# State-space stage: input projections of x, B and C as seven half-size products from the third group on

## The reference, cut to what matters

```python
zxbcdt = x @ w_in                      # x: 256 x 1024; w_in: 1024 x 6176
z = zxbcdt[..., :2048]
xbc = zxbcdt[..., 2048:2048 + 4096]    # x: 2048 columns, B: 1024, C: 1024
dt_raw = zxbcdt[..., 6144:]
xbc = silu(causal_depthwise_conv(xbc, conv_w, conv_b))   # 4 taps along the tokens
xs, bm, cm = xbc[..., :2048], xbc[..., 2048:3072], xbc[..., 3072:]
...
y = ssd_chunked(xh, dt, a, bm, cm) + d_skip * xh         # per group: 4 heads of 64, state 128, 2 chunks of 128
yg = y * silu(z); yg = yg * rsqrt(mean(yg ** 2, per group) + eps)
out = yg @ w_out
```

## Time and profile before

| | before |
|---|---|
| median of 3 runs | 1808.0 us |
| span of the profiled execution | 1806.1 us |
| TensorE busy | 1786.0 us, 99% |
| VectorE busy | 721.9 us, 40% |
| ScalarE busy | 448.2 us, 25% |
| GpSimd busy | 70.9 us, 4% |
| HBM read | 524.91 MB, 291 GB/s over the span |

### The profile page before, as it was taken

How to read it: one execution, slowest core, us unless ns; L and a number is a source line. 1 busy time by engine, 2 the same in 40 slices (tenths; PEclk the granted TensorE clock), 3 DMA queues, 4 the chain that set the end, 5 groups by cost and what they waited for, 6 DMA issues and landing times.

```text
span 1806.1 us, 21261 instructions
## 1 busy us (share of the span) xinstructions
PE 1786.0 (99%) x8612; PEld 984.0 (54%) x8647; DVE 721.9 (40%) x1667; ACT 448.2 (25%) x958; POOL 70.9 (4%) x66
## 2 busy tenths in 40 slices
PE   9999999999999999999999999999999999999999
PEld 8888754443443333455444344343366767568874
DVE  3566754212221213035421221221345566234675
ACT  2332312111111100133210111110134534217780
POOL 0000000000000000000000000000011110001110
PEclk9999999999999999999999999999999999999999
DMA  9723569999999999708899999999942332041520
GB/s 389 305 83 139 193 254 410 420 427 428 426 428 429 427 427 425 309 1 349 357 425 428 428 427 427 428 427 427 425 162 94 140 123 110 7 181 47 236 91 23
DMA packets 41828, 527.41 MB, mean 292 GB/s; under 512 B 4800, under 2 KB 5472, under 8 KB 8576
## 3 DMA queue, kind: packets, MB, share of 16 engines
q1 hardware_dynamic: 39200, 516.70, 68.7%
q10 hardware_dynamic: 2528, 9.31, 1.3%
HBM read 524.91 MB, written 1.08 MB: 291 GB/s over the span
## 4 chain that ended last, share of the span: by engine, by line
PE 88%; DMA 9%; DVE 2%; SPq 1%; ACT 0%; issue 0%; POOL 0%; DVEq 0%; ACTq 0%
PE ps L212 32%; PE ps L876 20%; PE ps L911 10%; DMA ring<-in_wu 6%; PE ps L810 4%; PE ps L928 3%; PE ps L715 2%; DMA ring<-in_w_lat 2%; PE ps L1702 2%; PE ps L1670 2%; PE ps L1234 1%; PE ps L679 1%; PE ps L1717 1%; PE ps L883 1%; PE ps L1446 1%; PE ps L1459 1%
## 5 line engine op out<-in xcount | busy, mean ns | idle before, releaser
L876 PE MATMUL ps<-ring,work 128*64 128x512 f32 x1856 | 409.1, 593 | 6.0 <-DMA ring<-in_wu 5.7
L212 PE MATMUL ps<-xl,ring 128*128 128x256 f32 (+3 forms) x1344 | 291.5, 375 | 0.4 <-DMA ring<-in_w_x 0.4
L876 PEld LDWEIGHTS ps<-ring,work 128*64 128x64 f32 x1856 | 131.6, 137 | 270.7 <-issue 251.2
L212 PEld LDWEIGHTS ps<-xl,ring 128*128 128x128 f32 x1344 | 243.7, 190 | 39.5 <-issue 2.5
L911 PE MATMUL ps<-ring,work 128*64 128x512 f32 x816 | 181.5, 594 | 0.1
L212 PE MATMUL ps<-ring,xl 128*128 128x256 f32 (+1 forms) x576 | 176.0, 463 | 0.2 <-ACT xl L1787 0.2
L2647 DVE TENSOR_TENSOR work<-work,ps 128x512 f32<-128x512 f32 x32 | 22.0, 688 | 361.4 <-PE ps L876 341.7
L212 PEld LDWEIGHTS ps<-ring,xl 128*128 128x128 f32 x576 | 108.3, 190 | 59.3 <-issue 49.9
L911 PEld LDWEIGHTS ps<-ring,work 128*64 128x64 f32 x816 | 56.2, 137 | 100.3 <-issue 98.7
L3178 POOL TENSOR_TENSOR small<-small,halves 128x1 f32<-128x1 f32 (+4 forms) x42 | 45.7, 1087 | 1545.7 <-DVE small L2449 936.6
L2608 DVE SCALAR_TENSOR_TENSOR work<-ps,small,big 128x512 f32<-128x512 f32 x60 | 45.0, 750 | 135.8 <-ACT big L1918 135.8
(11 more groups left out here) (476 smaller groups left out, 1958.9 us busy)
## 6 DMA issues: line engine op xcount, KB each, us to landing
ring<-in_wg SPq DMA_DIRECT2D x62, 2048.0 KB, 20.6
ring<-in_wu SPq DMA_DIRECT2D x52, 2048.0 KB, 21.7
ring<-in_wd SPq DMA_DIRECT2D x48, 2048.0 KB, 22.0
xl<-in_wd SPq DMA_DIRECT2D x10, 2048.0 KB, 23.5
xl<-in_wu SPq DMA_DIRECT2D x9, 2048.0 KB, 19.1
ring<-in_w_odd SPq DMA_DIRECT2D x8, 2048.0 KB, 7.4
ring<-in_w_xz SPq DMA_DIRECT2D x7, 2048.0 KB, 22.9
ring<-in_w_qkv SPq DMA_DIRECT2D x6, 2048.0 KB, 34.3
```

The lines of the kernel that those rows point to most:

```text
L212: i = e.matmul(bout, lhs(k), rhs(k), start=start and k == ks[0], stop=stop and k == ks[-1])
L876: last = e.matmul(b[64 * j:64 * j + 64, :], x[:, 4 * a + k, 64 * j:64 * j + 64], w[k // 2][:, 2 * (k % 2) + j, :], start=a + k == 0, stop= ...
```

## The change

The two blocks of a half, the two halves of the 256 tokens and the two halves of the 1024 features form a 2 x 2 by 2 x 2 product of matrices. From the third group on (`FAST = 2`) it is made of seven half-size products in place of eight (Winograd's form), each of 4 matmuls with 128 moving columns in place of 256: 28 matmuls of half the width per half, where there were 16.

- **GpSimd** makes the four sums of x once (`pool_x_sums`), and for each half four sums of weights of 512 elements a row, two groups ahead (`pool_sums`), one of them in place in the ring. They stand in its queue ahead of the power that y's norm needs.
- **TensorE** makes three products into ps5 (`part_mm`), then four into ps2 or ps3 (`mm_conv`). The first three of a half wait for `first_sums` of the half before, since they share ps5.
- **VectorE** adds the products up: copy and sum out of ps5, then three sums with the other bank, into `raw` in SBUF, and convolves from `raw` back into the products' bank. In the groups 1 to 6 the convolution of half 0 stands behind the decay products now, and in the groups 0 to 6 the second block of half 1 behind the gate.
- **ScalarE** takes the SiLU from the banks, one half at a time, for the groups from the third on.
- **The ring** gives one slot ("half") to the sums, from the start until `mm_conv(7, 1)`. "sum" is given out later, and the output weights are loaded in another order. What the loads near the seam of mixer and experts wait for:

| chunk, in SyncE's order before | waited for | waits for now |
|---|---|---|
| wo(0,0) | z of group 3 | the same |
| wo(1,1) | z of 4 | half 1 of 5 (third now) |
| wo(0,1) | half 1 of 5 | z of 4 (second now) |
| wo(1,0) | z of 5 | z of 6 |
| mg(0,0) | z of 6 | half 1 of 7 |
| mu(0,0), mu(0,1) | half 1 of 7, z of 7 | the same |
| md(0,0) | p5 | c21 |
| mg(1,0) | c21 | p7 |
| mg(1,1) | p3 | p3, behind mg(1,0) |
| mu(1,0), 1536 KB of it | z of 7 | the same, behind the others |
| mu(1,1) | p7 | p5, behind the others |
| md(1,0), then the first half of mg(0,1) | p4, p4 | the same |

From md(1,1) on the first layer's loads wait for the same steps of the experts as before.

```diff
+FAST = 2
...
+            if g == 1:
+                ring.add(("half",), 0, mm_conv(7, 1))
+                ring.order.remove(ring.chunks["half",][0])
+        WO = [(0, 0, "c21"), (0, 1, "p7"), (1, 1, "p3"), (1, 0, "p4")]
         for hf, n, last in WO:
+            if (hf, n) == (1, 0):
+                ring.add(("sum",), 0, out_mm("p5"))
             ring.add(("wo", hf, n), 1, out_mm(last))
+        ring.order.insert(1, ring.chunks["half",][0])
...
+        halfv = ring.view("half")
+        wsums = [area(halfv, 1536 * i, (3, 4, 128)) for i in range(2)]
+        xsums = [area(xl, 2048, (4, 128)), area(xl, 2560, (4, 128)), area(halfv, 3072, (4, 128)), area(halfv, 3584, (4, 128))]
+        raw = area(big, 3584, (4, 128))
+        def wq(g, half, j, h_):
+            v = kview(8, 512)(ring.view("BC", g // 2) if half else ring.view("w", g))
+            c = 256 * j + 128 * (g % 2) if half else 256 + 128 * j
+            return v[:, 4 * h_:4 * h_ + 4, c:c + 128]
+        def xq(h_, c):
+            return xS[:, 4 * h_:4 * h_ + 4, 128 * c:128 * c + 128]
...
+            if half < 2 and g >= FAST:
+                tensor_seven(e, g, half, j)
+            elif half < 2:
...
+        def tensor_seven(e, g, half, j):
+            x, y = ps[5], ps[2 + half]
+            s1, s2, s4 = (wsums[half][:, i] for i in range(3))
+            t1, t2, t3, t4 = xsums
+            def product(b, at, w, x_):
+                for k in range(4):
+                    last = e.matmul(b[:, 128 * at:128 * at + 128], w[:, k, :], x_[:, k, :], start=k == 0, stop=k == 3)
+                return last
+            if j == 0:
+                e.wait_ge(*(ring("BC", g // 2) if half else ring("w", g)))
+                if half:
+                    e.wait_ge(*first_sums(g, 0))
+                else:
+                    e.wait_ge(*(first_sums(g - 1, 1) if g > FAST else dec_d(0, 1)))
+                product(x, 0, wq(g, half, 0, 0), xq(0, 0))
+                product(x, 1, wq(g, half, 0, 1), xq(1, 0))
+                e.wait_ge(*sums_in(g, half))
+                product(x, 2, s2, t2).then_inc(*part_mm.up(g, half))
+            else:
+                e.wait_ge(*(cs_in(g - 1) if g > FAST else conv(g - 1, half)))
+                product(y, 1, s1, t1)
+                product(y, 2, wq(g, half, 1, 0), t3)
+                product(y, 0, wq(g, half, 1, 1), t4)
+                product(y, 3, s4, xq(1, 1)).then_inc(*mm_conv.up(g, half))
...
-            e.wait_ge(*conv(g, 1))
-            if g > 1:
-                e.wait_ge(*mm_off(g - 2))
-            e.activation(cs[:, g % 2], cv, ACT.Silu).then_inc(*cs_in.up(g))
+            if g < FAST:
+                e.wait_ge(*conv(g, 1))
+                e.activation(cs[:, g % 2], cv, ACT.Silu).then_inc(*cs_in.up(g))
+                return
+            e.wait_ge(*mm_off(g - 2))
+            for half in range(2):
+                e.wait_ge(*conv(g, half))
+                i = e.activation(cs[:, g % 2, 2 * half:2 * half + 2].rearrange("p a n -> p (a n)"), ps[2 + half][:, :], ACT.Silu)
+                i.then_inc(*(cs_in.up(g) if half else as_.up()))
...
-        def vector_conv(e, g, half):
-
+        def vector_conv(e, g, half, blocks=(0, 1)):
+            if g >= FAST and 0 in blocks:
+                x = ps[5][:, :].rearrange("p (a n) -> p a n", a=4)
+                y = ps[2 + half][:, :].rearrange("p (a n) -> p a n", a=4)
+                e.wait_ge(*part_mm(g, half))
+                e.tensor_copy(raw[:, 1], x[:, 0]).then_inc(*vs.up())
+                e.wait_ge(*vs())
+                e.tensor_tensor(raw[:, 0:4:2], bc(raw[:, 1], 1, 2), x[:, 1:3], ALU.add).then_inc(*first_sums.up(g, half))
+                e.wait_ge(*first_sums(g, half))
+                e.wait_ge(*mm_conv(g, half))
+                e.tensor_tensor(raw[:, 1:4:2], bc(raw[:, 2], 1, 2), y[:, 1:3], ALU.add).then_inc(*vs.up())
+                e.wait_ge(*vs())
+                e.tensor_tensor(raw[:, 1], raw[:, 1], y[:, 3], ALU.add).then_inc(*vs.up())
+                e.tensor_tensor(raw[:, 2:4], bc(raw[:, 3], 1, 2), y[:, 0:2], ALU.add).then_inc(*vs.up())
+                e.wait_ge(*vs())
             e.wait_ge(*mm_conv(g, half))
             if g:
                 e.wait_ge(*cs_in(g - 1))
-            for j in range(2):
+            for j in blocks:
                 blk = 2 * g + j if half == 0 else 16 + 8 * j + g
-                b = ps[2 + half][:, j * 256:(j + 1) * 256]
-                o = cv[:, 2 * half + j, :]
+                b, o = ps[2 + half][:, j * 256:(j + 1) * 256], cv[:, 2 * half + j, :]
+                if g >= FAST:
+                    b, o = raw[:, 2 * j:2 * j + 2].rearrange("p a n -> p (a n)"), b
...
-                if g < 7:
-                    vector_conv(e, g + 1, 0)
                 if g == 0:
+                    vector_conv(e, 1, 0)
                     for t in range(2):
                         e.wait_ge(*mm_seg(t))
                         e.tensor_tensor(dec[:, t], ps[4 + t][:, :].rearrange("p (h l) -> p h l", h=4),
...
                     e.wait_ge(*dec_e(g, t))
                     e.tensor_tensor(dec[:, t], dec[:, t], bc(ps[1][:, 128 + 128 * t:256 + 128 * t], 1, 4),
                                     ALU.mult).then_inc(*(vs.up() if t == 0 else dec_in.up(g)))
+                if 0 < g < 7:
+                    vector_conv(e, g + 1, 0)
                 if g < 7:
-                    vector_conv(e, g + 1, 1)
+                    vector_conv(e, g + 1, 1, (0,))
                 else:
                     vector_mix(e)
                 e.wait_ge(*mm_y(g))
...
                 e.wait_ge(*vs())
                 e.wait_ge(*zs_in(g))
                 e.tensor_tensor(yv, yv, zs[:, i], ALU.mult).then_inc(*gated.up(g))
+                if g < 7:
+                    vector_conv(e, g + 1, 1, (1,))
...
+        def pool_x_sums(e):
+            t1, t2, t3, t4 = xsums
+            e.wait_ge(x_in[0], 16)
+            e.wait_ge(x_in[1], 16)
+            e.wait_ge(*mm_conv(0, 1))
+            e.tensor_tensor(t1, xq(0, 1), xq(0, 0), ALU.subtract).then_inc(*gs.up())
+            e.wait_ge(*gs())
+            e.tensor_tensor(t2, xq(1, 1), t1, ALU.subtract).then_inc(*gs.up())
+            e.tensor_tensor(t3, xq(1, 1), xq(0, 1), ALU.subtract).then_inc(*gs.up())
+            e.wait_ge(*gs())
+            e.tensor_tensor(t4, xq(1, 0), t2, ALU.subtract).then_inc(*sums_in.up("x"))
+        def pool_sums(e, g, half):
+            s1, s2, s4 = (wsums[half][:, i] for i in range(3))
+            e.wait_ge(*(ring("BC", g // 2) if half else ring("w", g)))
+            e.wait_ge(*mm_conv(g - 1, half))
+            e.tensor_tensor(s1, wq(g, half, 1, 0), wq(g, half, 1, 1), ALU.add).then_inc(*gs.up())
+            e.wait_ge(*gs())
+            e.tensor_tensor(s2, s1, wq(g, half, 0, 0), ALU.subtract).then_inc(*gs.up())
+            e.tensor_tensor(wq(g, half, 1, 0), wq(g, half, 0, 0), wq(g, half, 1, 0), ALU.subtract).then_inc(*gs.up())
+            e.wait_ge(*gs())
+            e.tensor_tensor(s4, wq(g, half, 0, 1), s2, ALU.subtract).then_inc(*sums_in.up(g, half))
         def gpsimd(e):
+            pool_x_sums(e)
             for g in range(8):
+                if g + 2 < 8:
+                    for half in range(2):
+                        pool_sums(e, g + 2, half)
```

More of the change, by code:

```diff
@@ L279, in build @@
         qkT_in = Sig(sem("qkT_in"), qkT_mm.keys)
-        sc_mm, sc_max, sc_exp = sig("sc_mm", H8, range(2)), sig("sc_max", H8), sig("sc_exp", H8, range(2))
+        part_mm = sig("part_mm", range(FAST, 8), range(2))
+        first_sums = sig("first_sums", range(FAST, 8), range(2))
+        sc_mm, sc_max, sc_exp = then(part_mm, H8, range(2)), then(first_sums, H8), sig("sc_exp", H8, range(2))
         p_in, pT_mm, pT_in, av_mm, av_in = (sig(n, H8) for n in ("p_in", "pT_mm", "pT_in", "av_mm", "av_in"))
-        sl_var, sl_rs, sl_in = (sig(n, range(2), range(2)) for n in ("sl_var", "sl_rs", "sl_in"))
+        sums_in = Sig(sem("sums_in"), [("x",)] + each(range(FAST, 8), range(2)))
+        sl_rs = then(sums_in, range(2), range(2))
+        sl_var, sl_in = (sig(n, range(2), range(2)) for n in ("sl_var", "sl_in"))
         oT_mm, oT_in = sig("oT_mm", range(2), range(2)), sig("oT_in", range(2), range(2))
```

3 lines of the change are left out of this document (removed).

## The result

| | before | after |
|---|---|---|
| median | 1807.6 us | 1820.7 us (1819.6 to 1821.2) |
| span of the profiled execution | 1806.1 us | 1819.1 us |
| VectorE busy | 721.9 us | 748.0 us |
| GpSimd busy | 70.9 us | 136.5 us |

What follows compares the result with a forecast made beforehand. TensorE was taken to bound the mixer, only just, with VectorE's chain at no slack, and DMA the first expert layer. Mixer -7.9 + 1.2 + 4.5 + 2.2 = 0.0, seam +8: 1808.0 + 8 = 1816.0 us, range 1806 to 1825.

Steps and rivals of the forecast that it cites:

- TensorE's products: Mixer, groups 2 to 7: 56 half-width records take 6.25 us a half, saving 0.66 us in each of 12: -7.9 us.
- The rival of the weight loads: Mixer's products: weight loads bound the narrow matmuls at 0.125 us a record, mixer 9 us worse, 1825; chance 0.14.
- The estimate from the Trainium skill: Mixer's products: 25 ns added to each of 672 records, 16.8 us more, 1833; chance 0.03 within the weight loads' 0.14.
- VectorE's chain: Mixer, groups 1 to 6: added sums less covered waiting for ScalarE, net +0.2 us a group, +1.2 us.
- GpSimd beside it: Mixer: VectorE waits for GpSimd's fourth sum, 0.8 us in groups 1 to 5, 0.5 in group 0: +4.5 us.
- The first rival: Mixer: only GpSimd yields and VectorE loses nothing; mixer gains -4.5, seam costs 8, 1811.5 us; chance 0.20.
- The long sums: Mixer, groups 5 and 6: the 3584-element sum delays first_sums, so TensorE waits 1.1 us ahead of half 1: +2.2 us.
- The mixer: Sum of the mixer's terms: 0.0 us, between -4.5 (no waiting for GpSimd) and +9 (0.125 us a record).
- The seam: Mixer to experts: loads issued later make the first expert layer end later, +8 us, between 6.2 and 9.7.
- the 8.2 of the sum: First expert layer: the stream of weights runs 8.2 us late, and the layer ends with the stream.
- the early wait: Seam: TensorE waits 5.4 us at the first half of mg(0,1) and 0.8 at the second: 6.2 us.
- The rival of the other side: Seam: stream not late, seam costs nothing; 1803.5 us with GpSimd harmless, 1808 otherwise; chance 0.13.

Runs made afterwards that it cites:

- fourth_free: seam_gates with GpSimd's fourth sum for half 1 moved behind the next group's last decay operation: 1801.7 us, 0.9969 of the kernel before.
- sum_split: seam_gates with the 3584-element sums of groups 5 and 6 cut into two of 1792, the second behind half 0's convolution: 1806.4 us.
- free_split: fourth_free with the 3584-element sums also cut in two as in sum_split: 1802.1 us, 0.9967 of the kernel before.
- aside_first: The changed kernel with both halves of mg(0,1) issued ahead of mu(1,1) and md(1,0): 1815.5 us, 1.0041 of the kernel before.
- beside_late: The changed kernel with ScalarE's 1024 KB load into lnb issued later, behind the SiLU of pair 0: 1817.8 us.
- warm50: The changed kernel with 50 matmuls of a constant in TensorE's idle time ahead of the wait for mg(0,1)'s halves: 1818.1 us.
- seam_gates: The changed kernel with slots ordered so that the experts' first loads wait for the same steps as before: 1807.1 us, 0.9997 of the kernel before.
- ring_only: The kernel before with only the order of the weight slots changed, products, GpSimd and convolution as before: 1821.7 us, 1.0079 of before.

## Why the prediction was right, and where its steps were off

The sign, the two places and both mechanisms held; the seam's size did not.

- **TensorE's products, -7.9 us.** Right: 6.26 us a half against 6.25. The rival of the weight loads falls: 56 records in 6.26 us are 0.112 us each, 4 ns more than half of the 0.216 of 256 columns. The estimate from the Trainium skill ("TensorE: Matmul & The Clock Gate", Back-to-back issue gap), 1833, falls with it: it added 25 ns a record, which these rows don't show.
- **VectorE's chain, +1.2, and GpSimd beside it, +4.5.** Together 5.7, measured 4.9 us of gaps in the groups 0 to 5, none in group 6, where 0.2 was expected. All of the 4.9 is GpSimd's: fourth_free has none of it left, and its groups take 23.7 us where those of before took 25.1, so the chain's own 1.2 us did not come. The convolution into PSUM costs what it did (0.55 and 1.53 us). L2479 lost 0.91 us where I had put 0.8, at the operation and to the sum that the prediction named. fourth_free gives 5.4 us back. The first rival, that GpSimd costs nothing, falls.
- **The long sums, +2.2.** Two gaps of 1.0 us, 2.1 in all. As a place it was right; as a cause it was half the story, since sum_split and free_split show that the same time is owed at the end of the chain.
- **The mixer, 0.0.** Measured -1.0, as -7.9 + 4.9 + 2.1 = -0.9 gives it.
- **The seam, +8: the step that failed.** "What TensorE doesn't lose at 278 us it loses where it meets the queue" is borne out by aside_first, which puts the stream at 8.4 us against the 8.2 of the sum (in an order that itself holds mu(1,1) back, so the match is in part luck). But that makes the seam the larger of early wait and stream, and the early wait was sized at 6.2, where 11.7 us and 2.9 us of clock were measured, above the 9.7 of my upper bound. Four things are missing in the 6.2. The kernel waits for both halves in one wait, so by the forecast's own times it waits from 277.87 to 285.7, 7.8 us: +1.6. The second half landed at 288.6 instead of 285.7, +2.9; the load of ScalarE, which the sum of landings left out, is worth about that: without it the half lands 3.4 us earlier in beside_late. TensorE arrived at 277.05, +0.8. These make 11.5 of the 11.7. And the clock, +2.9, which warm50 gives back. The prediction's reason for the later loads, "a slot less", falls too: seam_gates has a slot less as well and no wait at the seam. It is the order of the slots that counts.
- **The rival of the other side**, a stream that is not late, falls by ring_only; seam_gates shows what it would have given, 1807.1, near its 1808.
- **The total.** The span is 1819.1 against the 1814.1 of the forecast, 5.0 us more: 6.7 missing at the seam, less 1.0 gained in the mixer and 0.7 gained elsewhere, which no run traces. The range had its room above for a dearer GpSimd and for slow weight loads; that it held a dearer seam is luck.

## What to carry to other kernels

When the slots of a ring are given out anew, write down for every load what it now waits for, and sum up the landings with every queue's loads in. Here a burst of four big loads ahead of a smaller one that was needed first cost 14.7 us, more than the 7.9 that the faster matmuls gained, and not because a slot was missing. The late stream cost the larger of its first wait and its lag, so mending the first wait alone (aside_first) gives back 5 us of 13; here the other gates for the same loads gave back all. And before work is given to an idle GpSimd, look at which VectorE operations work in SBUF alone while it runs, and at the one that its own result releases: the same sum cost 5 us beside L2481, 5 us beside `y_norm`'s products and nothing behind the decays.
